# SiLU of a DeltaNet head's q, k, v and z by one ScalarE function, with a table swap in each head

## What is computed

```python
c, new_gdn_conv = _causal_dwconv(g_qkv, gdn_conv_buf, gdn_conv_w)   # 4 taps
c = jax.nn.silu(c)
gq, gk, gv = jnp.split(c, [GDN_QK, 2 * GDN_QK], axis=-1)
gq = _l2norm(heads(gq, GDN_HEADS, GDN_DK)) * (GDN_DK ** -0.5)
gk = _l2norm(heads(gk, GDN_HEADS, GDN_DK))
...
go, new_gdn_S = _gated_delta_chunked(gq, gk, gv, g, beta, gdn_S)
go = _rmsnorm(go.transpose(0, 2, 1, 3), gdn_norm_w) * jax.nn.silu(g_z)
```

## Time and profile before

| | us |
|---|---|
| median of 3 runs | 2030.31 (2029.37 to 2030.98) |
| the profiled execution's own time | 2027.79 |
| its span in the profile | 2025.6 |

### The profile page before, as it was taken

The page is one execution under the profiler, slowest core; times in us unless marked ns, Lnnn a source line. Parts: engine busy times, 40 slices in busy tenths (PEclk is TensorE's granted clock), DMA queues, the critical chain, the costliest instruction groups (busy, mean ns, idle before and its releaser), DMA issues.

```text
span 2025.6 us, 39152 instructions
## 1 busy us (share of the span) xinstructions
PE 1952.9 (96%) x14427; PEld 1896.6 (94%) x14427; DVE 1209.8 (60%) x2417; ACT 936.3 (46%) x1846; POOL 200.2 (10%) x311
## 2 busy tenths in 40 slices
PE   6899999999999999999999999999999999999997
PEld 4789999999999999999989999999999999999996
DVE  3756656666664555546655566764466764466753
ACT  4434444454444444445554454443354443444533
POOL 4102111211110010110012100000000000000032
PEclk9999999999999999999999999999999999999999
DMA  7444545455445756655557566666556666566551
GB/s 164 115 114 133 148 128 149 133 133 140 136 131 153 186 151 169 170 144 160 178 148 198 136 161 164 166 166 166 166 156 162 161 160 168 167 166 167 155 146 64
DMA packets 566395, 307.87 MB, mean 152 GB/s; under 512 B 6379, under 2 KB 561475, under 8 KB 565971
## 3 DMA queue, kind: packets, MB, share of 16 engines
q1 hardware_dynamic: 523691, 278.22, 51.0%
q10 hardware_dynamic: 42400, 27.88, 4.8%
q0 software_dynamic: 192, 0.26, 0.2%
HBM read 293.32 MB, written 13.02 MB: 151 GB/s over the span
## 4 chain that ended last, share of the span: by engine, by line
PE 79%; DVE 7%; ACT 5%; issue 5%; POOL 2%; DMA 1%; ACTq 1%; DVEq 0%; POOLq 0%; SPq 0%
PE products L1689 23%; PE products L1691 22%; PE products L1690 22%; DVE w_lo L521 2%; ACT w_hi L514 2%; PE mixer L1669 2%; PE products L1669 1%; POOL sig L629 1%; PE mixer L1770 1%; PE mixer L1776 1%; PE mixer L1777 1%; PE mixer L1885 1%; DVE conv_out L1347 1%; DVE u_gate L1604 1%; DVE u_val L1604 1%
## 5 line engine op out<-in xcount | busy, mean ns | idle before, releaser
L521 DVE TENSOR_TENSOR w_lo<-w_raw,w_hi 128x512 fp32r<-128x512 f32 x1037 | 722.6, 710 | 706.5 <-ACT w_hi L514 703.8
L514 ACT ACTIVATE w_hi<-w_raw 128x512 fp32r<-128x512 f32 x1037 | 632.4, 627 | 664.9 <-PE products L1691 632.1
L1689 PE MATMUL products<-h_hi,w_hi 128*128 128x288 f32 x1536 | 481.1, 313 | 7.4 <-DVE w_lo L521 5.4
L1691 PE MATMUL products<-h_hi,w_lo 128*128 128x288 f32 x1536 | 458.1, 298 | 0.0
L1690 PE MATMUL products<-h_lo,w_hi 128*128 128x288 f32 x1536 | 457.9, 298 | 0.0
L1689 PE MATMUL products<-f_hi,w_hi 128*128 128x288 f32 x1408 | 418.4, 297 | 1.0 <-ACT r L1106 1.0
L1691 PE MATMUL products<-f_hi,w_lo 128*128 128x288 f32 x1408 | 418.0, 297 | 0.0
L1690 PE MATMUL products<-f_lo,w_hi 128*128 128x288 f32 x1408 | 414.7, 295 | 0.0
L1689 PEld LDWEIGHTS products<-h_hi,w_hi 128*128 128x128 f32 x1536 | 293.1, 191 | 22.8 <-DVE w_lo L521 11.3
L1690 PEld LDWEIGHTS products<-h_lo,w_hi 128*128 128x128 f32 x1536 | 293.0, 191 | 0.5
L1691 PEld LDWEIGHTS products<-h_hi,w_lo 128*128 128x128 f32 x1536 | 291.5, 190 | 0.0
(11 more groups left out here) (431 smaller groups left out, 2348.4 us busy)
## 6 DMA issues: line engine op xcount, KB each, us to landing
w_raw<-in_w_in SPq DMA_DIRECT2D x96, 1024.0 KB, 6.0
w_raw<-in_w_up SPq DMA_DIRECT2D x88, 1024.0 KB, 5.9
w_raw<-in_w_down SPq DMA_DIRECT2D x32, 1024.0 KB, 5.9
w_raw<-in_w_out SPq DMA_DIRECT2D x16, 1024.0 KB, 7.8
w_raw<-in_w_down SPq DMA_DIRECT2D x16, 768.0 KB, 4.9
w_raw<-in_w_branch_a SPq DMA_DIRECT2D x8, 1024.0 KB, 5.4
w_raw<-in_w_branch_b SPq DMA_DIRECT2D x8, 1024.0 KB, 5.3
S_sample<-in_state_gdn_S ACTq DMA_DIRECT2D x8, 512.0 KB, 4.2
```

The costliest lines, as they stand in the source:

```text
L514: nc.scalar.activation(ring_slot(whi, whi2, n, ring), raw[:, s % slots, 4 * j:4 * j + 4], ACT.Copy).then_inc(hi_ready, 1)
L521: nc.vector.tensor_tensor(ring_slot(wlo, wlo2, n, ring), raw[:, s % slots, 4 * j:4 * j + 4], ring_slot(whi, whi2, n, ring).bitcast(F32), A ...
L1689: mm(out, w_hi, x_hi, start=start, stop=False)
L1691: return mm(out, w_lo, x_hi, start=False, stop=stop)
```

## The change

- `prepare` on ACT: in slot 3 the table set of Silu is loaded; once DVE's `cv23` is done, two ACTIVATEs write Silu of `cv` straight into `qkv` (768 and 96 columns). In slot 4 a third makes Silu of `z` in place, and the set `EXP_LN` is loaded back.
- The three ACTIVATEs on `sig`, both clamps, POOL's product of `z` and DVE's two products are gone, and the tile `sig` with them. `rn` and `sq`, which lay in `sig`'s place, have places of their own.
- `sq` on POOL is issued in slot 5 instead of 7 and waits for ACT's `si2`. DVE's slot 7 waits for `si2` instead of its own product. DVE's slot 10 waits for `sq` as well.

```diff
@@ prep steps
-        prep_a = Steps(sem("prep_act"), "c0 c1 c2 lr sg1 sg2 sg3 d1 d2 ..."
+        prep_a = Steps(sem("prep_act"), "c0 c1 c2 lr si1 si2 sz d1 d2 ..."
@@ gpsimd, prepare(h)
-                yield 3
-                pool.wait_ge(*prep_d.after("cv23", h))
-                pool.wait_ge(*prep_a.before(h))
-                pool.wait_ge(*prep_t.before(h))
-                apart(pool)
-                pool.tensor_scalar(sg[:, 0:3 * GV], cv[:], SIG_MIN, None, ALU.max).then_inc(*prep_p.done("clamp"))
-                yield 6
-                pool.wait_ge(*prep_a.after("sg3", h))
-                apart(pool)
-                pool.tensor_tensor(z[:], z[:], sg[:, 3 * GV:], ALU.mult).then_inc(*prep_p.done("zz"))
-                yield 7
-                pool.wait_ge(*prep_d.after("qkv2", h))
-                pool.wait_ge(*prep_p.after("zz", h))
+                yield 5
+                pool.wait_ge(*prep_a.after("si2", h))
                 pool.tensor_tensor(sq[:], qkv[:, 0:2], qkv[:, 0:2], ALU.mult).then_inc(*prep_p.done("sq"))
@@ scalar, prepare(h)
                 yield 3
-                act.wait_ge(*prep_d.after("clampz", h))
-                act.wait_ge(*prep_p.after("clamp", h))
-                nc.scalar.activation(sg[:], sg[:], ACT.Exp, scale=-1.0).then_inc(*prep_a.done("sg1"))
+                nc.scalar.preload_act_table(ACT.Silu)
+                act.wait_ge(*prep_d.after("cv23", h))
+                cv3 = cv[:].rearrange("p (t g) -> p t g", t=3)
+                nc.scalar.activation(qkv[:, :, 0:TP], cv3[:, :, 0:TP], ACT.Silu).then_inc(*prep_a.done("si1"))
+                nc.scalar.activation(qkv[:, :, TP:T].rearrange("p t (b s) -> p t b s", s=L), spaced(cv3[:, :, GPAD + TP:], GS),
+                                     ACT.Silu).then_inc(*prep_a.done("si2"))
                 yield 4
-                act.wait_ge(*prep_a.after("sg1", h))
-                nc.scalar.activation(sg[:], sg[:], ACT.Ln, bias=1.0).then_inc(*prep_a.done("sg2"))
-                yield 5
-                act.wait_ge(*prep_a.after("sg2", h))
-                nc.scalar.activation(sg[:], sg[:], ACT.Exp, scale=-1.0).then_inc(*prep_a.done("sg3"))
+                nc.scalar.activation(zt[h % 3][:], zt[h % 3][:], ACT.Silu).then_inc(*prep_a.done("sz"))
+                nc.scalar.preload_act_table_set(EXP_LN)
@@ vector, prepare(h)
-                dve.wait_ge(*in_place("g", h))
-                d("clampz", ts(sg[:, 3 * GV:], zt[h % 3][:], SIG_MIN, None, ALU.max))
-                yield 6
-                dve.wait_ge(*prep_a.after("sg3", h))
-                step(prep_d, f"cv2{GC - 1}", h)
-                cv3, sg3 = ...
-                d("qkv1", tt(qkv[:, :, 0:TP], cv3[:, :, 0:TP], sg3[:, :, 0:TP], ALU.mult))
-                d("qkv2", tt(qkv[:, :, TP:T]..., spaced(cv3[:, :, GPAD + TP:], GS), spaced(sg3[:, :, GPAD + TP:], GS), ALU.mult))
                 yield 7
                 dve.wait_ge(grow_in, 16 * (h + 1))
-                step(prep_d, "qkv2", h)
+                dve.wait_ge(*prep_a.after("si2", h))
...
                 yield 10
                 dve.wait_ge(*prep_a.after("rn2", h))
+                dve.wait_ge(*prep_p.after("sq", h))
```

More of the change, by code:

```diff
@@ L227, in build @@
         gq = [sx.put(f"gdn_qkv{i}", [P, 3, GW]) for i in range(2)]
[L228 to L232, removed]
+        rn = sx.put("rn", [P, 2, T])
+        sq = sx.put("sq", [P, 2, T])
         qkv = sx.put("qkv", [P, 3, T])
@@ L318, in build @@
         old_p = Steps(sem("gdn_old_pool"), "put")
-        prep_a = Steps(sem("prep_act"), "c0 c1 c2 lr sg1 sg2 sg3 d1 d2 rn1 rn2 kg0 kg1 x0a x0b kg2 psb1s "
+        prep_a = Steps(sem("prep_act"), "c0 c1 c2 lr si1 si2 sz d1 d2 rn1 rn2 kg0 kg1 x0a x0b kg2 psb1s "
                        + " ".join(f"psb{l}" for l in LEVELS) + " psb6")
         prep_d = Steps(sem("prep_dve"), " ".join(f"cv{t}{j}" for j in range(1, GC) for t in range(3))
-                       + " clampz qkv1 qkv2 d0 d1 d2 bd1 bd2 k q ke qe bv0 bv1 bv2 at1 at2 n0a n0b xt1 xt2 pt1 pt2 n1a n1b n2 xx1s xx1 "
+                       + " d0 d1 d2 bd1 bd2 k q ke qe bv0 bv1 bv2 at1 at2 n0a n0b xt1 xt2 pt1 pt2 n1a n1b n2 xx1s xx1 "
                        + " ".join(f"n{l + 1} xx{l}" for l in LEVELS[1:-1]) + " xx5 xx6")
-        prep_p = Steps(sem("prep_pool"), "la lb clamp zz sq ec1 ec2 k4 x4")
+        prep_p = Steps(sem("prep_pool"), "la lb sq ec1 ec2 k4 x4")
         prep_t = Steps(sem("prep_pe"), "last norm tr kk kq x0 trs " + " ".join(f"p{l} xx{l}" for l in LEVELS) + " p6 xx6")
@@ L615, in prepare @@
             def prepare(h):
-                x4, xx, ec, g, z = handed[h % 2][0], *handed[h % 2][-2:], gq[h % 2], zt[h % 3]
+                x4, xx, ec, g = handed[h % 2][0], *handed[h % 2][-2:], gq[h % 2]
                 yield 0
@@ L1347, in prepare @@
                         d(f"cv{t}{j}", stt(c, gq[h % 2][:, t, j:j + GV], gcw[:, j, t * H + h:t * H + h + 1], c, ALU.mult, ALU.add))
-                dve.wait_ge(*in_place("g", h))
-                d("clampz", ts(sg[:, 3 * GV:], zt[h % 3][:], SIG_MIN, None, ALU.max))
-                yield 6
-                dve.wait_ge(*prep_a.after("sg3", h))
-                step(prep_d, f"cv2{GC - 1}", h)
-                cv3, sg3 = cv[:].rearrange("p (t g) -> p t g", t=3), sg[:, 0:3 * GV].rearrange("p (t g) -> p t g", t=3)
-                d("qkv1", tt(qkv[:, :, 0:TP], cv3[:, :, 0:TP], sg3[:, :, 0:TP], ALU.mult))
-                d("qkv2", tt(qkv[:, :, TP:T].rearrange("p t (b s) -> p t b s", s=L), spaced(cv3[:, :, GPAD + TP:], GS),
-                             spaced(sg3[:, :, GPAD + TP:], GS), ALU.mult))
                 yield 7
                 dve.wait_ge(grow_in, 16 * (h + 1))
-                step(prep_d, "qkv2", h)
+                dve.wait_ge(*prep_a.after("si2", h))
                 for n, t0, c in PARTS:
```

## The result

The changed kernel takes 2020.1 us (median of 4 runs, 2016.4 to 2021.4) against 2030.6 (4 runs) for the kernel before: a ratio of 0.9948, 95% interval 0.9932 to 0.9963. A second set of runs gave 2019.4 (6 runs) against 2030.3 (17 runs), ratio 0.9957 (0.9944 to 0.9969). So the change saves 9 to 11 us, 0.4 to 0.5%, and the two intervals together allow 6 to 14 us; 2021.4 was forecast, 8.9 us less than before.

The account below looks back on a forecast made before the run. PE was taken to set the time, with room on ACT and DVE on average. Savings of 3.8 us (heads 1 to 7) and 5.1 (head 0) sum to 8.9, from 2030.3 to 2021.4 us; the forecast's own range is 2018 to 2024.

Parts of the forecast that it names:

- The swap: ACT, two table loads per head: 1.30 us each, 2.6 us per head.
- (c): Every head: a swap costs twice its row, 2.57 us, delaying `ks_sample`; 2024.4 us, or 2025.7 with the skill's drain; chance 0.06.
- (d): Every head: a swap amid traffic costs far more than in a quiet place; at 4 us each 2045.8 us; chance 0.04.
- The ACTIVATEs: ACT's Silu on 768, 96 and 288 columns: 0.85, 0.28 and 0.45 us, 1.6 us per head.
- Heads 1 to 7: PE's waits for POOL's `sq` go, while `ks_sample` stays in time: 3.8 us saved, bounds 3 to 5.
- Head 0: DVE's chain to the scaled k and q shortens, so PE's transposes start earlier: 5.1 us saved, bounds 2 to 6.5.
- the lower bound: Head 0: saving of only 2 us if POOL's contention comes back elsewhere and the next `w_lo` is held.
- The second half: Heads 1 to 7: they may reach their bound of 5 us saved.
- rival (b): PE's clock stays up in head 0 and heads 1 to 7 reach their bound of 5: 2018.3 us; chance 0.10.
- Its first half: Head 0: a shorter first wait leaves PE's clock up, so some 14 matmuls of 0.13 us, 1.9 us, come back.
- Rival (a): Only `sq` pays; in head 0 DVE's small operations, `w_lo` or PE's clock catch the gain: 2026.5 us; chance 0.15.
- (e): `sq` wasn't last: PE's wait passes to another late step in slot 9, row operations hold head 0; 2030 us; chance 0.05.

## Why the prediction was right

**The swap.** Forecast 1.30 us each; the loads are 1.283 with 0.01 to 0.02 behind them. In the run with four more, five loads in a row still took 1.29 each. Two more loads moved `ks_sample` by 2.6 us against the Silu of `z`, four by 5.15; in the kernel before it was 2.7 with the lost overlap of two ACTIVATEs. That overlap is also why ACT became busier by 0.8 us per head and not by the 0.5 of the forecast, as far as I can tell; with PE as the bound it cost nothing visible. The drain of 1.38 us of the Trainium skill (ScalarE: Activation LUTs, What ACT_TABLE_LOAD costs) is in none of the traces; rivals (c) and (d) are out, and the run with two more loads shows where they would have begun: at 2.6 us more behind `ks_sample` PE just starts to wait, 0.2 to 0.5 us.

**The ACTIVATEs.** Forecast 0.85, 0.28 and 0.45 us; measured 0.846, 0.275 and 0.435. The three-dimensional view cost nothing.

**Heads 1 to 7.** From the end of slot 3's weights copy, forecast and measured: next copy 2.2 and 2.25 us, copy of slot 5 at 4.8 and 4.86, `ks_sample` done at 6.2 and 6.29, margin 2.3 and 2.25. The wait for `sq` went entirely. The one term that was mis-sized is its price: 3.8 us forecast (bounds 3 to 5), 5.4 measured, 0.8 a head, which lies above the upper bound. I summed PE's idle time. A product's row ends 0.30 us after its start while the next could start after 0.13, so each wait hides 0.17 us, 1.2 of the missing 1.6 us in seven heads. The idle time of the weight loads for the same wait was nearer:

```profile
PEld mixer L1731 <- POOL sq L637: 5.4, 7, 1.0
```

The run with two more loads bears this out: for `ks_sample` PE was idle 1.3 us in all, the weight loads 2.9, and heads 1 to 7 grew by 2.8.

**Head 0.** From the end of the taps, forecast and measured: copy of slot 4 after 1.0 and 1.0 us, copy of slot 5 after 3.7 and 3.6, `w_lo` behind it after 4.4 and 4.3. The transposes start 17.8 us after the taps where it was 23.2, in both profiles of either kernel: 5.4 us, forecast 5.1. Contention with POOL did come back elsewhere, as the lower bound feared, but small: the `w_lo` beside `sq` takes 1.16 us instead of 0.69. That PE's own gain would be swallowed by a longer wait at the transposes was right as well:

```profile
89.10 0.40 PE L1667 MATMUL products<-h_hi,w_hi 128*128 128x288 f32 x1 [0.60 <-DVE w_lo L518]
91.33 0.40 PE L1667 MATMUL products<-h_hi,w_hi 128*128 128x288 f32 x1 [0.37 <-DVE w_lo L518]
93.60 0.37 PE L1667 MATMUL products<-h_hi,w_hi 128*128 128x288 f32 x1 [0.40 <-DVE w_lo L518]
106.22 1.33 PE L1647 MATMUL mixer<-ident,qkv 128*128 128x128 f32 x5 [5.02 <-DVE qkv L1351]
```

Rows 8 had 3.19 and 4.21 us; now it is three short waits, 1.4 us in all where two of about 1 us were forecast, and 5.02. In the second profile of the kernel before the wait at the transposes is 2.6 us and the one for `sq` 2.1 instead of 0.9, with the transposes in the same place behind the taps: DVE's chain sets them, not PE. The shorter first wait did keep the clock up until PE stood waiting for the transposes, but it brought nothing, since PE only arrived earlier at the wait for DVE. The second half of rival (b) came true, as heads 1 to 7 gained more than its 5 us, with the clock at 1.00 in them before and after. Its first half is out, since behind the wait at the transposes the clock is low again:

```profile
106.00:111.00 5.00, 4.78 (x21) 4.43 (x22) 4.52 (x14) 1.62 (x5) 0.32 (x1) 0.50 0.44 42
```

Rival (a), only `sq` pays, is out with head 0's 5.2 us, and (e) with the absence of any `sq` wait.

**What the prediction didn't see** is that the function named in the change is hardly what pays. It priced the clamp's leaving and Silu's shorter chain as one. By stages the kernel without clamps is 9.9 us shorter than the one before with the old function, the changed one 10.6. The forecast of the time doesn't rest on that split, so it was not right by luck: its steps were measured where it expected them, but for the price of the wait for `sq`.

## What to carry over

When an in-order engine waits, ask who holds it: here the expensive part of the sigmoid was not its three passes on ScalarE but one clamp on GpSimd ahead of them, and taking that away is worth nearly as much as a new function with two table swaps. Price a table swap by where it stands in its engine's queue: 2.6 us per head cost PE no wait where 2.3 us of margin were left behind them, and a wait of 2.1 to 2.2 us per head where the margin had been 0.4 to 0.5. And count a PE wait by the idle time of the weight loads, or by the gap between starts, since the row of a product of 288 columns hides the first 0.17 us of it here.

## What the runs showed of the hardware beyond that

The clock's recovery behind a wait of PE differs between profiles of one program. PE waits 3.6 us for `mix_lo` in all ten profiles, and the stretch to the first `f_hi` is 23.2 and 25.6 us in the kernel before, 25.5 and 23.1 in the changed one, and 21.7 to 25.4 in the others. The shortest is the kernel before with late loads, where the clock did not fall at all; it lies outside the 23 to 26 us that had been expected:

```profile
1047.00:1062.00 15.00, 11.51 (x81) 10.68 (x82) 8.66 (x16) 8.25 (x17) 0.64 (x1) 1.00 0.44 124
```

In single profiles this noise of 3.9 us is over a third of the effect studied here, which is why the stages were compared and not the spans.

Nor does the length of a wait tell, in this range, whether the clock falls. It fell behind three of seven waits of 2.1 to 2.2 us (`ks_sample` in the kernel before with late loads), behind four of seven waits of 2.7 to 2.8 us (the changed kernel with four more loads), and behind nine of ten waits of 3.6 us (`mix_lo`). Behind the seven of 0.2 us with two more loads it stayed up. What decides it between 2 and 4 us no run here shows.
